# A second buffer for the right-hand sides of the linear stages, and sample tokens stacked by heads for the top-k search, with two of its operands in PSUM

## What is computed

```python
h = rms_norm(x) * (1 + scale1) + shift1
q, k, v, qi, ki, wi, u_conv, gates = split(h @ w_in)
attn = sparse_attention(q, k, v, qi, ki, wi)          # top-k keys, softmax
y = silu(layer_norm(depthwise_conv(a * sigmoid(g))))
g_attn, g_conv = split(sigmoid(gates))
merged = g_attn * (attn @ w_o_attn) + g_conv * (y @ w_conv_out)
x = x + gate1 * (merged @ w_out)
h2 = rms_norm(x) * (1 + scale2) + shift2
# PEER: product-key experts, 8 heads, 2 halves of 128 sub-keys, 16384 experts
s1, s2 = (h2 @ w_q_peer) . sub_keys1, (h2 @ w_q_peer) . sub_keys2
v1, i1 = top_k(s1, 16); v2, i2 = top_k(s2, 16)
top_s, top_j = top_k(v1[:, None] + v2[None, :], 16)   # of 256 pairs
eid = (i1 * 128 + i2)[top_j]; gate = softmax(top_s)
out = sum_k gate * gelu(u_emb[eid] . h2) * v_emb[eid]
```

## Time and profile before

| | |
|---|---|
| runs | 1296.15, 1297.43, 6810.18 us (median 1297.43) |
| the profiled execution | 1294.03 us |
| its span, first to last instruction | 1292.2 us |
| PE (TensorE) busy | 1238.0 us, 96% |
| PEld (weight load) busy | 1115.9 us, 86% |
| DVE (VectorE) busy | 964.2 us, 75% |
| ACT (ScalarE) busy | 572.4 us, 44% |
| POOL (GpSimd) busy | 564.0 us, 44% |
| granted TensorE clock, mean | 0.985 of full |
| chain that ended last | PE 77%, DVE 17%, DMA 2% |

### The profile page before, as it was taken

The page is one execution under the profiler, slowest core; times in us unless marked ns, Lnnn a source line. Parts: engine busy times, 40 slices in busy tenths (PEclk is TensorE's granted clock), DMA queues, the critical chain, the costliest instruction groups (busy, mean ns, idle before and its releaser), DMA issues.

```text
span 1292.2 us, 27745 instructions
## 1 busy us (share of the span) xinstructions
PE 1238.0 (96%) x8591; PEld 1115.9 (86%) x8591; DVE 964.2 (75%) x2397; ACT 572.4 (44%) x993; POOL 564.0 (44%) x272
## 2 busy tenths in 40 slices
PE   5999999989997999988999999999999999999998
PEld 3767677887997999988999999999888888888887
DVE  4499955855343999999699999950367888888876
ACT  2200144555444444454455555544455554545452
POOL 0100025430564567888666666667501344444100
PEclk8999999899998999999999999999999999999999
DMA  9866455344443346655555555556777898888863
GB/s 354 314 241 203 149 196 191 115 147 137 143 146 128 131 149 209 208 167 183 179 182 186 183 178 181 186 187 211 253 251 256 311 341 302 306 310 293 286 229 133
DMA packets 114442, 273.14 MB, mean 211 GB/s; under 512 B 31376, under 2 KB 54640, under 8 KB 114000
## 3 DMA queue, kind: packets, MB, share of 16 engines
q1 hardware_dynamic: 99200, 243.76, 54.5%
q0 software_dynamic: 6432, 19.71, 4.3%
q10 hardware_dynamic: 8752, 8.93, 2.1%
HBM read 249.30 MB, written 23.00 MB: 211 GB/s over the span
## 4 chain that ended last, share of the span: by engine, by line
PE 77%; DVE 17%; DMA 2%; SPq 1%; ACT 1%; issue 1%; ACTq 0%; POOL 0%; DVEq 0%; POOLq 0%
PE ps L2092 18%; PE ps L2095 9%; PE ps L1696 9%; PE ps L2036 7%; PE ps L2035 7%; PE ps L2042 7%; PE ps L1733 4%; PE ps L1739 4%; PE ps L1745 3%; PE ps L2071 2%; DVE big L1496 2%; DVE big L1490 2%; DVE big L1451 1%; DMA ring<-in_stream 1%; PE ps L1761 1%; DVE big L1498 1%
## 5 line engine op out<-in xcount | busy, mean ns | idle before, releaser
L665 POOL TENSOR_TENSOR split<-ring,split 128x1024 fp32r<-128x1024 f32 x128 | 326.8, 2557 | 134.3 <-ACT split L967 134.3
L967 ACT ACTIVATE split<-ring 128x1024 fp32r<-128x1024 f32 x256 | 271.5, 1061 | 174.5 <-PE ps L2092 168.2
L2035 PE MATMUL ps<-h2r,split 128*128 128x288 f32 x1024 | 279.0, 297 | 2.2 <-ACT split L967 2.2
L2036 PE MATMUL ps<-h2r,split 128*128 128x288 f32 x1024 | 279.1, 297 | 0.0
L2092 PE MATMUL ps<-h2r,split 128*128 128x512 f32 x1024 | 257.4, 392 | 1.4 <-DVE h2r L1585 1.4
L2092 PEld LDWEIGHTS ps<-h2r,split 128*128 128x128 f32 x1024 | 184.2, 189 | 34.5 <-ACT act L996 1.6
L2035 PEld LDWEIGHTS ps<-h2r,split 128*128 128x128 f32 x1024 | 192.9, 188 | 2.9 <-issue 2.2
L2036 PEld LDWEIGHTS ps<-h2r,split 128*128 128x128 f32 x1024 | 192.4, 188 | 0.0
L630 POOL TENSOR_TENSOR split<-ring,split 128x1024 fp32r<-128x1024 f32 x48 | 117.8, 2454 | 163.5 <-ACT split L763 162.7
L2042 PE MATMUL ps<-h2r,split 128*128 128x288 f32 x1024 | 157.8, 296 | 7.4 <-POOL split L665 6.8
L1591 DVE TENSOR_TENSOR split<-ring,split 128x1024 fp32r<-128x1024 f32 x128 | 156.1, 1220 | 0.1
(11 more groups left out here) (265 smaller groups left out, 1601.5 us busy)
## 6 DMA issues: line engine op xcount, KB each, us to landing
ring<-in_stream SPq DMA_DIRECT2D x379, 512.0 KB, 3.4
act_dram<-act SPq DMA_DIRECT2D x128, 128.0 KB, 1.7
parts<-act_dram SPq DMA_DIRECT2D x16, 512.0 KB, 4.7
big<-act_dram SPq DMA_DIRECT2D x16, 512.0 KB, 5.4
big<-in_stream SPq DMA_DIRECT2D x12, 512.0 KB, 11.7
big<-in_cache_k ACTq DMA_DIRECT2D x16, 128.0 KB, 3.4
big<-in_cache_v ACTq DMA_DIRECT2D x16, 128.0 KB, 3.1
s_act_dram<-act SPq DMA_DIRECT2D x128, 16.0 KB, 1.4
```

Of the source, the lines that this page charges most:

```text
L665: nc.gpsimd.tensor_tensor(split[:, n % 2, 1], ring[:, slot_of(n), :], split[:, n % 2, 0].bitcast(f32), ALU.subtract).then_inc(lo_ready, 1)
L967: nc.scalar.activation(split[:, n % 2, 0], ring[:, slot_of(n), :], ACT.Copy).then_inc(hi_ready, 1)
L2035: MM(out, u_hi[:, k], h_hi[:, k], start=(k == 0), stop=False)
L2036: last = MM(out, u_hi[:, k], h_lo[:, k], start=False, stop=False)
```

## The change

It has two parts. **Right-hand sides.** A second buffer `rhs_other` (`y_r`) lies over the start of `big`, where `hT` and `xn` were. The odd stages (`conv_out`, `out`) read it, the even ones `rhs_parts`. `y` is cut chunk by chunk behind the `gate_b` tiles, `attn` within the head loop (prompt columns per head, sample columns in one instruction at step 13 and 14), `ga` behind each `attn_out` tile. Squares that were kept in `xn` go to `y`. **Search.** The sample tokens' scores of heads h, h+2, ... are written to the four quarters of the partitions, so that 32 tokens x 4 heads fill 128 partitions; their units come in every second round only. The look-ups read their tables from PSUM. The lists for the sample gather are then already on the right partitions, and four DMAs on SyncE fall away. `BEFORE` and `SOFTMAX` are each 12 chunks earlier.

```diff
-BEFORE = 44
-SOFTMAX = 28
+BEFORE = 32
+SOFTMAX = 16
+HEADS = [PH] * NQ + [PH * TS // P]
+        with ExitStack() as over_big:
+            rhs_other = over_big.enter_context(nc.sbuf_tensor("y_r", [P, 2, KC * T], f32r))
+        place_ps = [adab[:, t * 2 * P:(t + 1) * 2 * P].rearrange("p (w k) -> p w k", w=2) for t in range(NQ)]
+        index_ps = [stb[:, t * 2 * P:(t + 1) * 2 * P].rearrange("p (h w a) -> p w h a", w=2, a=PTOP) for t in range(NQ)]
...
-            sp.wait_ge(s_picked, 2)
-            for q4 in range(4):
-                sp.dma_start(pick_at[q4 * TS:(q4 + 1) * TS], s_pick[0:TS, :, q4 * TS:(q4 + 1) * TS])\
-                    .then_inc(s_picks_in, 16)
...
+            def cut_rhs(parts, src, k, ready, value, n=T):
+                eng.wait_ge(ready, value)
+                nc.scalar.activation(parts[:, 0, k * T:k * T + n], src[:, k, 0:n], ACT.Copy).then_inc(rhs_hi, 1)
...
                 evac(("gate_b", n), gb[:, n], ACT.Sigmoid)
-            eng.wait_ge(tile_done, POS["gate_b", KC - 1] + 1)
-            cut_rhs(y, conv_ready, 1)
+                if n:
+                    cut_rhs(rhs_other, y, n - 1, conv_ready, n)
+            cut_rhs(rhs_other, y, KC - 1, conv_ready, KC)
...
+                    if m >= H:
+                        cut_rhs(rhs_parts, attn, m - H, mixed_copied, m + 1, TP)
...
-            cut_rhs(attn, s_mixed_copied, 0)
-            for n in range(1, KC):
-                cut_tile(("attn_out", n))
-            for n in range(2):
-                cut_tile(("out", n))
-            eng.wait_ge(tile_done, POS["attn_out", KC - 1] + 1)
-            cut_rhs(ga, merged, 1)
+            for n in range(1, KC + 2):
+                cut_tile(("attn_out", n) if n < KC else ("out", n - KC))
+                if n >= 2:
+                    cut_rhs(rhs_other, ga, n - 2, merged, n - 1)
...
+                if n >= H + 3:
+                    low_rhs(rhs_parts, attn, n - H - 3, 2, TP)
...
-                units = [(t, n) for t in range(NT) for n in range(4 * grp, 4 * grp + 4)]
+                units = [(t, n) for t in range(NQ) for n in range(4 * grp, 4 * grp + 4)]
+                if grp % 2:
+                    units += [(NQ, n) for n in (grp - 1, grp)]
...
-                for w in range(2):
-                    step(V.tensor_copy(tab[0:r, w, t], tab_u[0:r, w, t]))
+                step(V.tensor_copy(place_ps[t], tab_u[:, :, t, 0:HEADS[t] * PTOP]))
...
-                    step(V.tensor_tensor(eq[0:r], tab[0:r, w, t].unsqueeze(2).to_broadcast([r, PH * PTOP, PTOP]),
+                    step(V.tensor_tensor(eq[:, 0:n], place_ps[t][:, w].unsqueeze(2).to_broadcast([P, n, PTOP]),
...
+                rhs_h, rhs_l = (g_hi, g_lo) if stage % 2 else (h_hi, h_lo)
...
-                    for t in range(NT):
+                    for t in range(NQ):
+                    for j in range(4):
+                        q4 = (n - 3 + j) // 2 % 4
+                        last = MM((adab, stb)[n // 8][q4 * TS:(q4 + 1) * TS, j % 2 * NSUB:(j % 2 + 1) * NSUB],
+                                  qh[:, n - 3 + j, TP:T], sk[:, j % 2], start=True, stop=True)
```

More of the change, by code:

```diff
@@ L334, in build @@
         eq = late.take(PH * PTOP, PTOP)
-        s_expert = late.take(3, PH * PTOP)
+        s_expert = late.take(2, TS)
         assert late.at <= NSUB * TP
@@ L1265, in merge_conv, with low_rhs @@
                 V.tensor_tensor(gb[:, n], lin[BANK[key]][:, 0:T], gb[:, n], ALU.mult).then_inc(gated, 1)
+            def low_rhs(parts, src, k, stage, n=T):
+                part = slice(k * T, k * T + n)
+                dve.wait_ge(rhs_hi, stage * KC + k + 1)
+                V.tensor_tensor(parts[:, 1, part], src[:, k, 0:n], parts[:, 0, part].bitcast(f32), ALU.subtract)\
+                    .then_inc(rhs_lo, 1)
+            hi_all, lo_all = (rhs_parts[:, part].rearrange("p (k t) -> p k t", t=T) for part in range(2))
             def bias(n):
@@ L1416, in _ @@
                                        ALU.mult).then_inc(h2_ready, 1)
-            hi_all, lo_all = (rhs_parts[:, part].rearrange("p (k t) -> p k t", t=T) for part in range(2))
             dve.wait_ge(s_rhs_hi, 1)
@@ L1447, in _ @@
+                each(lambda t, n: V.match_replace(out=scw[:, t, n], in_to_replace=va[:, t, n, 0:8], in_values=sc[:, t, n],
+                                                  imm_value=TAKEN))
+                each(lambda t, n: V.max(out=va[:, t, n, 8:16], in_=scw[:, t, n]))
+                each(lambda t, n: V.max_index(out=ix[:, t, n, 8:16], in_max=va[:, t, n, 8:16], in_values=scw[:, t, n]))
                 settle()
-                units = [(t, h) for t in range(NT) for h in (2 * grp, 2 * grp + 1)]
+                units = [(t, h) for t in range(NQ) for h in (2 * grp, 2 * grp + 1)]
@@ L1450, in _ @@
+                if grp % 2:
+                    units.append((NQ, grp // 2))
                 nu = len(units)
[L1451 to L1455 removed]
@@ L1497, in _ @@
                     settle()
[L1498 removed]
+                    step(V.tensor_reduce(tsel[:, t, w, 0:n], eq[:, 0:n], AX.X, ALU.add))
                     settle()
@@ L1532, in _ @@
+            settle()
+            for w in range(2):
+                V.tensor_copy(pick_at[:, w], s_expert[:, w]).then_inc(s_picked, 1)
             step(V.tensor_copy(iota_ps, iota[:, :]))
@@ L1715, in _ @@
             h_hi, h_lo = (rhs_parts[:, part].rearrange("p (k t) -> p k t", t=T) for part in range(2))
+            g_hi, g_lo = (rhs_other[:, part].rearrange("p (k t) -> p k t", t=T) for part in range(2))
             def linear_cut(key, *halves):
@@ L1732, in linear_cut @@
                                 pe.wait_ge(rhs_hi, stage * KC + k + 1)
-                            MM(out, hi[:, k], h_hi[:, k], start=(k == 0), stop=False)
+                            MM(out, hi[:, k], rhs_h[:, k], start=(k == 0), stop=False)
                     if key == ("peer_q", 0) and half == 0:
                         pe.wait_ge(s_rhs_lo, 1)
+                    if key == ("attn_out", 0) and half == 0:
+                        pe.wait_ge(s_attn_lo, 1)
                     for k in range(half * KC // 2, (half + 1) * KC // 2):
@@ L1738, in linear_cut @@
                             pe.wait_ge(rhs_lo, stage * KC + k + 1)
-                        last = MM(out, hi[:, k], h_lo[:, k], start=False, stop=False)
+                        last = MM(out, hi[:, k], rhs_l[:, k], start=False, stop=False)
                 last.then_inc(lin_hi_used, 1) if 1 in (halves or range(2)) else None
@@ L1744, in linear_cut @@
                 for k in range(KC):
-                    last = MM(out, lo[:, k], h_hi[:, k], start=False, stop=(k == KC - 1))
+                    last = MM(out, lo[:, k], rhs_h[:, k], start=False, stop=(k == KC - 1))
                 last.then_inc(tile_done, 1)
@@ L2013, in _ @@
                     pe.wait_ge(act_evac, ACT_EVAC["peer_q", n])
-                    for t in range(NT):
-                        m = n // 4 * NT + t
-                        cols, rows = tokens(t)
+                    for t in range(NQ):
+                        m = n // 4 * NQ + t
+                        cols = tokens(t)[0]
                         if m >= 4:
```

188 lines of the change are left out of this document (90 added, 98 removed).

## The result

| | kernel before | changed kernel |
|---|---|---|
| device time, median of six runs (of the kernel before one took 6810.18 us) | 1296.04 us | 1273.26 us |
| span of the profiled execution | 1292.2 us | 1269.2 us |
| mean granted clock of the profiled execution | 0.985 | 0.991 |

The ratio is 0.9834, with a 95% interval of 0.9814 to 0.9855: 1.7% faster, within 2%.

A forecast was written before the change was run, and what follows sets the result against it. PE was taken as the bound, slowed in the score phase by VectorE and GpSimd holding each other up, and at three stage ends. Terms 3.0 + 3.1 + 2.9 - 1.0 + 10.5 = 18.5 us gave 1279 us, range 1272 to 1288.

The forecast's parts named there:

- conv_out, 3.0: Behind gate_b: the 2.17 us wait for the first softmax row goes, perhaps the low clock too; 3.0 us gained.
- my lower bound: For conv_out: a gain of 2.2 us if the low clock there stays; the upper bound was 3.7.
- attn_out, 3.1: First attn_out tile and the 0.71 us wait ahead of it: 3.1 us gained, between 1.9 and 3.6.
- the head loop, -1.0: Added cuts and subtractions in the head loop: 1.0 us lost, most of at most 4.8 hidden.
- out, 2.9: First out tile: 2.9 us gained; at most 3.6, lower bound 1.5 if low parts too are waited for.
- At nothing: Terms priced at zero: earlier mixing, four fewer DMAs on SyncE, sample scores on quarters (12 products a round either way).
- Score phase, 10.5: Score phase: 11.4 us of slowed chunks plus the 1.6 wait, less 2.0 softmax delay and 0.5 remaining collisions: 10.5 gained.
- The margin of 15: Before chunk 28: selection ends at 546, PE wants the picks at 561; 15 us to spare, so no wait.
- The slower rival: Selection late: PE stops at chunk 28 for the picks; over 15 us late costs time, 34 makes it slower; 3%.
- That the stage ends give nothing: Rival: gains at the three stage ends are cancelled, only the score phase gains; 1287 us, 15%.
- That PSUM does not end the collisions: Rival: look-ups stay long, selection ends 4 us late, score phase gains about 1 us; 1288 us, 7%.
- More than forecast: Rival: all clock losses at the changed places go, loop additions and exp hidden; 24 us gained, 1273 us, 9%.

The follow-up runs named there:

- e2: The kernel before with the second right-hand side buffer alone; search, look-ups and deadlines as before: 1290.44 us, ratio 0.9955.
- e1: The kernel before with the search part alone (stacked sample heads, tables in PSUM, earlier deadlines), one right-hand side buffer: 1281.27 us, ratio 0.9887.
- e9: The changed kernel with all sample score products written to one quarter of the partitions (wrong scores): 0.42 us more a round; only PE's times read.
- e3: The changed kernel with the four look-up tables back in SBUF, nothing else: 1285.67 us, ratio 0.9916 to the kernel before.
- e7: The kernel before with its four look-up tables in PSUM, nothing else: 1282.49 us, ratio 0.9912.
- e11: The changed kernel with look-up tables in SBUF and the old deadlines (BEFORE 44, SOFTMAX 28): 1279.03 us, ratio 0.9874 to the kernel before.
- e5: The changed kernel with BEFORE 28 instead of 32, SOFTMAX still 16: 1280.98 us, ratio 0.9906 to the kernel before.
- e6: The changed kernel with three orders altered (softmax exp behind a cut, last group's copy earlier, sample products 0, 2, 1, 3): 1270.91 us, ratio 0.9820.

## Why the prediction held, step by step

The forecast summed to 18.5 us against the profile of before; the kernels differ by 18.6 at equal clock and by 23.0 in span. The 3.9 us ahead of the changed lines hang on the two executions. The agreement at equal clock is partly luck: the forecast had 8.0 us for the right-hand sides and 10.5 for the search part, and alone they give 5.0 (e2) and 13.8 (e1). The errors of 3 us each have opposite signs. The median is 5.7 us below the 1279.0 because that of the kernel before came out 1.4 lower than the 1297.43 that the forecast started from, and because the changed kernel's runs had the higher clock (0.989 against 0.985).

*conv_out, 3.0.* The wait of 2.17 is gone, and the products after it run at 1.32 us instead of 2.29: 7.25 us from the end of `gate_b` to `conv_out` became 5.25, and 1.0 more in the products, 3.0 in all. The 2.17 did not come back whole, as PE has a new idle stretch of 0.79 ahead of L1970 (first block of the result; 0.7 in e2, none with one buffer). These products need VectorE's copy L1272, and that now stands beside GpSimd's low cuts of `y`, which begin 6.8 us earlier:

```profile
261.59 0.87 DVE L1272 COPY big<-ident 32x256 f32<-32x256 f32 x1
...
259.47 6.80 POOL L654 TENSOR_TENSOR y_r<-big,y_r 128x288 fp32r<-128x288 f32 x8
```

Before, this copy (L1258) started at 263.97, ahead of the low cuts (266.30), and took 0.27. So the first part of the change brings a small collision of the kind that the second part takes away; the sum had no term for it, and no run tests it alone. But e1 shows the 1.0 missing with one buffer as well; in e2, with two, `conv_out`'s first product comes 0.8 us earlier than e1's although this run's `gate_b` ended 0.8 later, a gain of 1.6. A sound price is 1.6 to 2, at or below my lower bound, and a share of the low stretches, which are rarer with two buffers.

*attn_out, 3.1, and the head loop, -1.0.* From the end of `conv_out`'s first eight products (274.83 by the earlier trace rows, and 267.96) to the second `attn_out` tile (336.92, and 328.28) 1.8 us were gained where the two terms give 2.1. The first tile runs at full pace, 328.28 - 325.02 = 3.26. The stretch between the first `conv_out` and the first `attn_out` product takes 58.4 us, and 58.3 in e1, which has one buffer, no low clock there and the wait of 0.71 in it. So the loop and the copy together lost 0.8, 0.44 of it the copy of the last group (a wait of 1.07 instead of 0.63), which the forecast had named. Again 1.5 us of the tile's gain was the clock of one run.

*out, 2.9.* Measured 2.2: the first tile takes 355.41 - 350.68 = 4.73 us. This term was too large. PE waits 0.61 for the last cut and 0.18 for the low part, and idles as much again between records: 1.5 us are lost in the tile where I had 0.7. What the lower bound was given for, low parts that are waited for too, is seen in the second of these waits.

*At nothing.* The sample scores on quarters gave 4 x 0.42 = 1.7 us (e9); a longer low stretch at `peer_q` took a part of it back, and 1.4 us were gained between the second `out` tile and the scores. This is the step that was wrong in kind. It happens to make up for `out`.

*Score phase, 10.5.* Measured 10.8. Look-ups at 2.29, low cuts at 2.40, no wait for the picks and the softmax delay kept (a wait of 1.61): all as forecast. The Trainium skill, page "SBUF — State Buffer", section "SBUF: two separate sides", has the lock for this; e3, e7 and e11 agree with it, and so do the colliding remains. They are seen in the changed kernel in operations on SBUF alone:

```profile
416.45 4.35 DVE L1476 TENSOR_TENSOR big<-big 128x256 f32<-128x256 f32 x4
...
542.80 2.28 DVE L1536 TENSOR_TENSOR big<-fold,iota 128x32 f32<-128x32 f32 x1
```

*The margin of 15.* It was 7: the picks are made at 542.4, and PE's transposes of them start at 549.51. The search took 500.24 - 406.96 = 93.3 us where 82 + 7 = 89 had been forecast, since the pair adds collide in every round now, the first included (4.35 us for four in the first; six took 2.09 there before), and 7.5 us passed to the first look-up instead of 4.5. The slower rival was nearer than its 3% said: e5 stands four chunks further and pays 4.8 us at equal clock.

*The rivals.* That the stage ends give nothing falls by e2. That PSUM does not end the collisions falls by e7 and e3. "More than forecast" named the clock, which is the cause of the rest, but at the changed places; most of it came from a place that the change does not touch. The Trainium skill, page "TensorE: Matmul & The Clock Gate", Part 1, has the slow clock as the resting state that activity releases. The low stretch at `peer_q` stands around a wait of 4.5 us in every profile and agrees with it; the one at 231 to 236, also in every profile, begins within or right behind 64 small products with only a wait of 0.7 ahead of them, so a wait alone does not tell where the clock falls. How far the change itself raises the clock stays open: the means are 0.985 to 0.987 for the three kernels with one buffer and 0.985 to 0.989 for the eight with two.

## What to carry to other kernels

Two engines that stretch each other show up as busy, not as waiting: compare the quickest and the median duration of one instruction form, and if the operands' place explains the difference, move the operand (small tables here) before shortening the work. Price a change in pieces that can be undone singly; here the place of the tables gave 11.4 us, the second buffer 5, and the large rewrite of the search, with the earlier deadlines, 2.3. Before crediting a gap in a trace to the code, look whether the clock was low in it, and take a second profile of the same kernel: executions of the kernel before lie up to 12.6 us apart, and their clocks with them.

## What was not expected of the hardware

- Matrix products with 32 weight columns that write different quarters of the partitions take 0.08 us apiece, those that write the same quarter 0.13; whether neighbours or next but one alternate made no difference (e6).
- A plain copy behind an exp had a table load of its own, 1.28 us, and a gelu behind it another; ahead of the exp it needs none.
- A VectorE operation on 32 columns took 2.28 us beside a low cut of GpSimd (L1536), one of 512 columns 2.81 where 0.69 is its work (e3): a short operation can pay for nearly the whole of the long one.
- The time of a run follows its mean granted clock by 9.5 us for each 0.01, and the low stretches moved between executions of the same kernel. Behind a wait of 4.8 us for the picks the clock stood at half for 3.4 us and cost 1.5 (e5).
